# Attention scores from 64-row halves of TensorE, issued in pairs, in place of full-height products with zero-padded queries

## The reference

```python
# block 1: differential attention, 4 heads, two maps of width 64 each, values of width 128
s = jnp.einsum("bqhmd,bkhmd->bhmqk", q, k).astype(jnp.float32) * (DA_QK_DIM ** -0.5)
p = jax.nn.softmax(s, axis=-1)
a = p[:, :, 0] - lam * p[:, :, 1]
return jnp.einsum("bhqk,bkhe->bqhe", a.astype(v.dtype), v)

# block 2, each of two layers: neighbourhood attention, 8 heads of width 64, with a position bias
s_loc = ... * scale + bias
s_ctx = jnp.einsum('bhqd,bhld->bhql', q_r, k_ctx).astype(jnp.float32) * scale
p = jax.nn.softmax(jnp.concatenate([s_loc, s_ctx], axis=-1), axis=-1)
```

## Time and profile before

| | |
|---|---|
| time, median of 3 runs | 4432.33 us (4431.28 to 4434.04) |
| span of the profiled execution | 4431.8 us |
| PE busy | 3617.5 us, 82% |
| PEld busy | 2466.8 us, 56% |
| DVE busy | 1528.5 us, 34% |
| ACT busy | 1051.3 us, 24% |
| POOL busy | 378.1 us, 9% |
| mean granted TensorE clock | 0.899 |

### The profile page before, as it was taken

The page is one execution under the profiler, slowest core; times in us unless marked ns, Lnnn a source line. Parts: engine busy times, 40 slices in busy tenths (PEclk is TensorE's granted clock), DMA queues, the critical chain, the costliest instruction groups (busy, mean ns, idle before and its releaser), DMA issues. The chain is left out here.

```text
span 4431.8 us, 42110 instructions
## 1 busy us (share of the span) xinstructions
PE 3617.5 (82%) x16570; PEld 2466.8 (56%) x16570; DVE 1528.5 (34%) x2849; ACT 1051.3 (24%) x1803; POOL 378.1 (9%) x216
## 2 busy tenths in 40 slices
PE   3997767577772897858999889999498868997998
PEld 0334554222221686637666468888386646655886
DVE  1112742100003256575111243333264663113444
ACT  1000421111113223324111142221332323113221
POOL 0000000100001223000211000000133001210000
PEclk7998868798896998879999989999799979998999
DMA  7762005599996211000210321211421002223222
GB/s 308 278 255 79 1 1 144 210 397 397 396 396 205 92 40 39 6 1 33 92 57 19 120 80 57 67 58 57 150 73 37 10 1 96 86 95 105 95 94 77
DMA packets 213103, 531.94 MB, mean 120 GB/s; under 512 B 8674, under 2 KB 46968, under 8 KB 202176
## 3 DMA queue, kind: packets, MB, share of 16 engines
q1 hardware_dynamic: 188992, 405.66, 25.7%
q0 software_dynamic: 17520, 85.53, 6.1%
q10 hardware_dynamic: 6416, 38.32, 2.2%
HBM read 486.71 MB, written 42.78 MB: 119 GB/s over the span
## 5 line engine op out<-in xcount | busy, mean ns | idle before, releaser
L483 PE MATMUL ps<-ring,hT 128*128 128x512 f32 (+1 forms) x1056 | 440.0, 577 | 12.6 <-DMA ring<-in_w_out_dram 10.3
L483 PEld LDWEIGHTS ps<-ring,hT 128*128 128x128 f32 x1056 | 197.5, 198 | 254.3 <-issue 251.4
L2149 PE MATMUL ps<-hT_hi,w_hi 128*128 128x512 f32 (+1 forms) x768 | 275.9, 359 | 20.5 <-DVE w_lo L2203 20.5
L2149 PE MATMUL ps<-hT_lo,w_hi 128*128 128x512 f32 (+1 forms) x768 | 276.4, 360 | 0.0
L2149 PE MATMUL ps<-hT_hi,w_lo 128*128 128x512 f32 (+1 forms) x768 | 275.9, 359 | 0.0
L1636 PE MATMUL ps<-wp_hi,hT_hi 128*128 128x512 f32 (+2 forms) x608 | 221.9, 365 | 64.8 <-POOL wp_lo L1615 64.8
L2155 PE MATMUL ps<-w_hi,h_lo 128*128 128x512 f32 x640 | 253.7, 396 | 0.0
L2155 PE MATMUL ps<-w_hi,h_hi 128*128 128x512 f32 x640 | 253.7, 396 | 0.0
L2155 PE MATMUL ps<-w_lo,h_hi 128*128 128x512 f32 x640 | 253.6, 396 | 0.0
L1636 PE MATMUL ps<-wm_hi,hT_hi 128*128 128x512 f32 x480 | 212.8, 443 | 37.3 <-POOL wm_lo L1919 37.3
L627 PE MATMUL ps<-pj,Z 128*128 128x64 f32 (+1 forms) x1856 | 237.4, 278 | 3.3 <-DVE hT L750 1.4
(11 more groups left out here) (357 smaller groups left out, 6028.3 us busy)
## 6 DMA issues: line engine op xcount, KB each, us to landing
pj<-in_expert_w_up_dram SPq DMA_DIRECT2D x32, 2048.0 KB, 21.7
pj<-in_expert_w_down_dram SPq DMA_DIRECT2D x32, 2048.0 KB, 20.4
ring<-in_expert_w_gate_dram SPq DMA_DIRECT2D x32, 2048.0 KB, 20.0
ring<-in_ffn_w_dram SPq DMA_DIRECT2D x64, 1024.0 KB, 5.3
Z<-in_w_mod_dram POOLq DMA_DIRECT2D x24, 2048.0 KB, 8.1
ring<-in_w_in_dram SPq DMA_DIRECT2D x42, 1024.0 KB, 5.3
pj<-in_w_ada_dram SPq DMA_DIRECT2D x12, 2048.0 KB, 17.3
ring<-in_w_in_dram SPq DMA_DIRECT2D x6, 2048.0 KB, 13.6
```

The costliest lines, as they stand in the source:

```text
L483: last = nc.tensor.matmul(bank(i % nb, w), lhs(k, t), s[:, k * w:k * w + w], start=(k == 0), stop=(k == nk - 1))
L2149: last = nc.tensor.matmul(bank(i % 8, c1 - c0), W[a][:, k, :], r[:, k, c0:c1], start=(k == 0 and r is hhk and a == 0), stop=(k == KT - 1 a ...
```

## The change

The zero-padded query copies go, and with them the memsets and the half copies. Queries lie in `qT` as the keys lie in `kT`. A score product takes 64 rows of both, the upper or the lower half. The two products of a pair are issued in turn, first both of 512 keys, then both of 256, each half into its own banks. In block 1 the pair is the two maps of one unit. In block 2 it is two heads of one query tile: the order of units is changed so that they are neighbours, both are issued at the even step, and the odd step issues no scores. Before the first product of a pair TensorE waits until both pairs of banks are free.

```diff
-        qz = [[Z[:, 1536:2304], Z[:, 2304:3072]], [hT[:, 4608:5376], hT[:, 5376:6144]]]
...
-                for m in range(A.nm):
-                    g = A.nm * i + m
-                    if g >= 2:
-                        pe.wait_ge(*A.free[g - 2])
-                    b = ps[:, 1024 * (g % 2):1024 * (g % 2) + 1024]
-                    rs = slice(*u["rows"][m])
-                    q = qT[u["head"] % 2]
-                    if A.split:
-                        q = qz[u["head"] % 2][rs.start // 64]
-                        rs = slice(0, P)
-                    q = q[rs, 128 * u["qt"]:128 * u["qt"] + 128]
-                    if len(u["keys"]) == 6:
-                        nc.tensor.matmul(b[:, 0:512], q, kT[u["head"] % 2][rs, 0:512], start=True, stop=True)
-                    nc.tensor.matmul(b[:, 512:768], q, kT[u["head"] % 2][rs, 512:768], start=True, stop=True).then_inc(s_done, 1)
+                if A.split:
+                    if A.nm == 1 and i % 2:
+                        return
+                    g = A.nm * i
+                    half = [slice(0, 64), slice(64, 128)]
+                else:
+                    g = i
+                    half = [slice(*u["rows"][0])]
+                for x in range(len(half)):
+                    if g + x >= 2:
+                        pe.wait_ge(*A.free[g + x - 2])
+                for c0, c1 in ((0, 512), (512, 768)) if len(u["keys"]) == 6 else ((512, 768),):
+                    for x, rs in enumerate(half):
+                        b = 1024 * ((g + x) % 2)
+                        last = nc.tensor.matmul(ps[:, b + c0:b + c1], qT[u["head"] % 2][rs, 128 * u["qt"]:128 * u["qt"] + 128],
+                                                kT[u["head"] % 2][rs, c0:c1], start=True, stop=True)
+                        if c1 == 768:
+                            last.then_inc(s_done, 1)
...
-            parts = [(slice(0, rows_), dst)]
-            if A.split and side == "q":
-                parts = [(slice(64 * x, 64 * x + 64), qz[h % 2][x][64 * x:64 * x + 64, 128 * ts[0]:128 * ts[-1] + 128]) for x in range(2)]
...
-            if A.split:
-                for b in range(2):
-                    for x in range(2):
-                        nc.vector.memset(qz[b][x][64 - 64 * x:128 - 64 * x, :], 0.0)
...
-                          y=pjt[:, t, NQ + 64 * h:NQ + 64 * h + 64]) for h in range(8) for t in TQ[l]]
+                          y=pjt[:, t, NQ + 64 * h:NQ + 64 * h + 64]) for q in range(4) for t in TQ[l] for h in (2 * q, 2 * q + 1)]
```

More of the change, by code:

```diff
@@ L651, in prep_out @@
             src = bank(7, 128 * len(ts))[0:rows_, :]
-            parts = [(slice(0, rows_), dst)]
-            if A.split and side == "q":
-                parts = [(slice(64 * x, 64 * x + 64), qz[h % 2][x][64 * x:64 * x + 64, 128 * ts[0]:128 * ts[-1] + 128]) for x in range(2)]
[L655 to L661, removed]
+            if who == "a":
+                last = nc.scalar.activation(dst, src, ACT.Copy, **({} if gain is None else {"scale": gain(side)}))
+            elif gain is None:
+                last = nc.vector.tensor_copy(dst, src)
+            else:
+                last = nc.vector.tensor_scalar(dst, src, gain(side), None, ALU.mult)
             last.then_inc(prep_a if who == "a" else prep_v, 1)
```

## The result

The changed kernel takes 4490.9 us (median, 4486.9 to 4492.8) against 4433.2 for the kernel before: 1.0125 times as long, 95% interval 1.0111 to 1.0140, so 58 us slower. The profiled execution lasts 4488.7 us, 56.9 more than the one of before.

A forecast was written before the change was run, and what follows sets the result against it. DA was taken as bound by TensorE and VectorE, both full, NA by a closed loop through ScalarE's copy behind the exponential. DA +1, NA +2 and clock +13 make +16 us on the 4432.3 median: 4448 us, range 4427 to 4471.

The forecast's parts named there:

- the term of the clock: NA0 and NA1: 2.1 us gaps bring 14.7 clock falls, 23.6 us, less 10 for today's falls; net +13 us.
- DA: Block 1 attention: loop 4.95 us a unit, waiting for both maps' exps; +1 us, bounds -1 and +4.
- the change of height: NA loop: going from 128-row to 64-row work costs 0 to 0.2 us a pair; +2 us, bounds 0 and +6.
- The pair of products: Scores in DA, NA0, NA1: halves overlap fully, a pair costs 1.34 instead of 2.68 us; 68 us TensorE work removed.
- Rival B: Score pairs: the halves don't overlap, up to 4489 us, or 4457 with half of the overlap; chance 0.09.
- The loop of NA: Block 2: transposes T, values V, score pair P; copy behind exp keeps 7.57 us for two units, no gain.
- Rival A: NA0 and NA1: same loops, the clock holds without falls; 4425 to 4435 us; chance 0.30.
- Rival C: NA: copy wait met in time, pairs at VectorE's 5.8 us; 57 us less, 4376 us; chance 0.08.
- The memsets and half copies: Stage starts: memsets worth 0 to 3.6 us, 1 taken; one query copy -0.6 us; both inside DA's +1.

The follow-up runs named there:

- the kernel with the filling: Changed kernel plus three extra full-height products (1.28 us) in the TensorE gap of full NA pairs, just ahead of the value matmuls; 4443.9 us.
- the 64-row filling: Changed kernel plus three extra products of 64 rows in place of 128 in the TensorE gap of full NA pairs; 4472.0 us.
- The fillings: Changed kernel with extra full-height products in the TensorE gap of full NA pairs: three products 4443.9 us, one product 4460.4 us.
- single 64-row products: Changed kernel, but in NA each unit's 64-row scores are issued in their own step with their own wait; DA keeps its pairs; 4524.6 us.
- the copy first: Changed kernel with ScalarE's copy of transposed tiles (unit i-2) ahead of the exponential of unit i, in all three attention kinds; 4377.9 us.

## Why the prediction was wrong

I forecast 4448 us in 4427 to 4471 and got 4491. The sign and the mechanism were right; the term of the clock was much too small. Of the 58 us the forecast had 16. The clock's term was 13 and came out at 41 in NA, DA's was 1 and came out at 5, the change of height was 2 and came out at 4. The last 7 or so lie in stages that the change doesn't touch.

*The pair of products.* Right. The halves overlap: 1.49 us for a pair. The working from the earlier trace rows was careless: four full-row records in 1.22 us make some 4.6 to 4.9 for 16, not 3.8, which speaks for overlap all the more. Rival B, products that do not overlap, gave 4489, close to the measured time, and was false in its mechanism. Only the trace tells the two apart.

*The loop of NA.* Right. 7.57 us plus 0 to 0.2 for the change of height was forecast, 7.69 measured in the kernel with the filling (7.70 in the changed one), with a gap of 1.98 (2.1 forecast) and the releaser as named. The Trainium skill, page "TensorEngine Tiling (Array Packing)", section "Key Properties", says that changing the tiling mode drains TensorE. The trace agrees that something is lost, 0.12 us a pair here and 0.41 more with the 64-row filling, but no record of it shows a drain.

*DA.* The loop was forecast at 4.95 and is 468.52 - 463.44 = 5.08 us, 0.13 more, which I did not take apart. The end of the idle time is the wait that the prediction named.

```profile
463.44 1.56 PE L597 MATMUL ps<-Z 64*128 64x512 f32 x8 [0.93 <-ACT Z L680]
...
468.52 1.56 PE L597 MATMUL ps<-Z 64*128 64x512 f32 x8 [1.15 <-ACT Z L680]
```

DA grew by 5.0 us, above the +4 bound of its term. The pitch makes 16 x (5.08 - 4.92) = 2.6 us of it. The rest goes with falls of the clock, which the prediction left out in DA: for 10.2 us from 440.1 and 3.4 from 453.8, beside gaps of 2.06 to 2.80 us ahead of P. From barrier to barrier the granted clock is 0.82 against 0.87, 42 us at the lower level against 29.

*The clock.* **This step failed, by size.** Forecast: 14.7 falls of 5.95 us, that is 87 us at the lower level, at 0.27 us each, 23.6 us, less 10 for today's four falls (24 us). Measured, the starts of the stages left out as in the forecast: 17 falls of 8.0 us on average, 136 us. From barrier to barrier it is 175 us at the lower level in place of 62, and 45 us more time. Both factors were small.

First, the time at the lower level. The number of falls was near the forecast, but four of the nine in NA0 stand at gaps of 2.35 to 2.94 us that end with the copy of a head's preparation (L656), a wait that the prediction doesn't price. In NA1 the falls lasted 5.95 us on average, exactly as taken over from before. In NA0 two lasted 20.5 and 27.3 us, over the small pairs. All four falls of the kernel before lay over small units too, and the longest was 10.2 us. Dense work without a gap did not bring the clock back in the 20.5 us, so the gap in every pair doesn't explain it, and what does stays open. With 136 us at the forecast's own price the term would have been 37 less 10, 27 us.

Second, the price. I let TensorE's own work set the pace at the lower level, 10.4 us a pair. But a fall that begins at the gap strikes T, V and P, which the loop holds, while the 4.05 us of VectorE and ScalarE in the loop do not shrink because TensorE is slow. An estimate from the loop's own terms with T, V and P at half speed is at most 4.05 + 2 x 1.97 + 2 x 1.55 = 11.1 us a pair (the fixed latencies in the 1.55 don't double), 3.5 us more, even where only those parts fall into the lower level. A pair of 10.91 us, seven tenths of it at the lower level, occurred twice in NA1. The fillings give 0.27 to 0.48 us for each microsecond at the lower level, 0.36 over all. With 113 us more of it, that is 41 us, and with 0.12 us for each of some 32 pairs, 4 us, it is the 45 that were measured.

*Rival A*, the clock holds, is near what the filled kernel shows: 4444 us against my 4425 to 4435, the excess being about what the pitch and DA make. The Trainium skill's page "TensorE: Matmul & The Clock Gate", in its section "Why this matters for your kernels", warns only of idle gaps longer than these. The measurement differs: the clock fell behind gaps of 1.98 us, less often when 0.43 us of work was put in, and in the middle of the stages not at all when 1.28 us was. The same page of the Trainium skill, in its section "A second HAM failure mode: psum-queue depth-cycling", describes what the windows show, a clock that swings with small idles between groups.

*Rival C* set its condition well: it decides from the point where the copy no longer stands behind the exponential. Moved there, NA runs at 6.08 us a pair, near VectorE's 5.8.

*The memsets and half copies* were not tried by themselves, so their share of the result isn't known.

## What to carry to other kernels

Follow the loop once around before pricing an edit: only what it holds once per turn can shorten it, and a product that is halved outside it turns into idle time. Idle time on TensorE is then not free, because it can take the clock down and so lengthen the parts that are in the loop. Where such a gap ends with one engine's instruction queued behind another of the same engine, look first at moving that one instruction. Here a copy moved ahead of an exponential gave 1% of the whole kernel, more than the cheaper matmuls gave with it or without it.

## What the runs showed of the hardware

Two streams of float32 products of 64 rows, 512 and 256 columns, into different banks overlap fully: 1.49 us for both, where one such stream alone took 1.48 (3540.59 - 3539.11, single 64-row products) and one of full height 1.34.

The granted clock answered to more than gaps. With 64-row score products that ran alone, TensorE was busy without a gap for 37.6 us and the clock stayed at its lower level, while the same units with 128-row products had 0.93 and 0.91 over the stages. Two halves beside one another are not cleared of this. With the copy first the clock was 0.92 and 0.93, but behind the start of NA1 no gap was over 0.9 us, so little was there to bring it down. In the changed kernel the falls of NA1, its start aside, ended after 6.8 us at most, and one in NA0 lasted 20.5 us with TensorE busy. What the chip measures is not settled by these runs.
